# FFN up projection of an fp32 decoder trunk: 18 of 22 gate/linear tile pairs by seven block products in place of eight

## The reference

```
D_MODEL = 1024
SEQ = 512
DEPTH = 4
FFN_HIDDEN = -(-8 * D_MODEL // (3 * 256)) * 256
...
def swiglu(h, w_gate_up, w_down):
    g, u = jnp.split(h @ w_gate_up, 2, axis=-1)
    return (jax.nn.silu(g) * u) @ w_down
...
        x = x + swiglu(rmsnorm(x, ffn_norm[i]), ffn_w_gate_up[i], ffn_w_down[i])
```

## Time and profile before

| | |
|---|---|
| median of 3 runs | 2382.03 us (2381.8 to 2382.3) |
| profiled execution, span | 2380.3 us |
| TensorE busy | 2370.0 us, 100% of the span, 11768 matmuls |
| weight loads busy | 2002.1 us, 84% |
| VectorE busy | 1332.7 us, 56% |
| ScalarE busy | 899.4 us, 38% |
| GpSimd busy | 310.5 us, 13% |
| memory read | 208.68 MB, 89 GB/s over the span |

### The profile page before, as it was taken

The page is one execution under the profiler, slowest core; times in us unless marked ns, Lnnn a source line. Parts: engine busy times, 40 slices in busy tenths (PEclk is TensorE's granted clock), DMA queues, the critical chain, the costliest instruction groups (busy, mean ns, idle before and its releaser), DMA issues.

```text
span 2380.3 us, 33586 instructions
## 1 busy us (share of the span) xinstructions
PE 2370.0 (100%) x11768; PEld 2002.1 (84%) x11768; DVE 1332.7 (56%) x2199; ACT 899.4 (38%) x1376; POOL 310.5 (13%) x305
## 2 busy tenths in 40 slices
PE   9999999999999999999999999999999999999998
PEld 7899988888888888888888888888889998888887
DVE  8667765344465764443586644446756676534444
ACT  6267833222233432222233322223426773322223
POOL 2211140000040120000033000003420114000003
PEclk9999999999999999999999999999999999999999
DMA  4710023232233232322233223233370002223232
GB/s 165 224 46 2 2 69 108 88 101 93 99 105 106 89 106 91 103 97 97 97 99 106 97 91 104 89 106 105 121 208 27 2 2 89 97 89 106 89 105 89
DMA packets 64616, 220.58 MB, mean 93 GB/s; under 512 B 7680, under 2 KB 7808, under 8 KB 64512
## 3 DMA queue, kind: packets, MB, share of 16 engines
q1 hardware_dynamic: 58320, 208.59, 26.3%
q0 software_dynamic: 5184, 8.40, 1.6%
q10 hardware_dynamic: 1008, 2.21, 0.3%
HBM read 208.68 MB, written 2.10 MB: 89 GB/s over the span
## 4 chain that ended last, share of the span: by engine, by line
PE 99%; DVE 0%; DMA 0%; ACT 0%; SPq 0%; issue 0%; DVEq 0%
PE bank L1516 95%; PE bank L1796 3%; DMA x<-x_in 0%; PE bank L1826 0%; DVE branch L1281 0%; DVE big L1509 0%; SPq L434 0%; DVE rden L1276 0%; ACT L588 0%; DVE w_lo L939 0%; DVE rden L1278 0%; ACT w_hi L572 0%; PE bank L1700 0%; ACT xs_hi L581 0%; ACT xg L907 0%
## 5 line engine op out<-in xcount | busy, mean ns | idle before, releaser
L1516 PE MATMUL bank<-xs_hi,w_hi 128*128 128x512 f32 (+1 forms) x1808 | 708.9, 392 | 1.1 <-DVE xs_lo L947 0.5
L1516 PE MATMUL bank<-xs_lo,w_hi 128*128 128x512 f32 (+1 forms) x1808 | 703.3, 389 | 0.0
L1516 PE MATMUL bank<-xs_hi,w_lo 128*128 128x512 f32 x1792 | 697.3, 389 | 0.0
L939 DVE TENSOR_TENSOR w_lo<-raw,w_hi 128x1024 fp32r<-128x1024 f32 x369 | 469.7, 1276 | 230.7 <-ACT w_hi L572 226.3
L572 ACT ACTIVATE w_hi<-raw 128x1024 fp32r<-128x1024 f32 x372 | 390.8, 1051 | 432.6 <-PE bank L1516 231.7
L1516 PEld LDWEIGHTS bank<-xs_hi,w_hi 128*128 128x128 f32 (+1 forms) x1808 | 339.0, 188 | 74.4 <-DVE xs_lo L947 1.5
L1516 PEld LDWEIGHTS bank<-xs_lo,w_hi 128*128 128x128 f32 (+1 forms) x1808 | 338.4, 187 | 71.0 <-issue 1.0
L1516 PEld LDWEIGHTS bank<-xs_hi,w_lo 128*128 128x128 f32 x1792 | 336.4, 188 | 70.0
L1516 PE MATMUL bank<-hid_hi,w_hi 128*128 128x512 f32 x720 | 280.5, 390 | 0.0
L1516 PE MATMUL bank<-hid_lo,w_hi 128*128 128x512 f32 x720 | 280.1, 389 | 0.0
L1516 PE MATMUL bank<-hid_hi,w_lo 128*128 128x512 f32 x720 | 280.1, 389 | 0.0
(11 more groups left out here) (212 smaller groups left out, 2719.8 us busy)
## 6 DMA issues: line engine op xcount, KB each, us to landing
raw<-stream SPq DMA_DIRECT2D x371, 512.0 KB, 3.2
w_f<-stream SPq DMA_DIRECT2D x18, 512.0 KB, 3.5
hid_hi<-mix_hi POOLq DMA_DIRECT2D x32, 128.0 KB, 3.7
hid_lo<-mix_hi POOLq DMA_DIRECT2D x32, 128.0 KB, 3.1
out<-big SPq DMA_DIRECT2D x8, 256.0 KB, 2.9
x<-x_in ACTq DMA_DIRECT2D x4, 256.0 KB, 6.8
x<-x_in SPq DMA_DIRECT2D x4, 256.0 KB, 7.5
big<-consts SPq DMA_DIRECT2D x1, 664.0 KB, 11.0
```

Of the source, the lines that this page charges most:

```text
L939: nc.vector.tensor_tensor(w_lo[:, slot, :], raw[:, k, :], f32(w_hi[:, slot, :]), ALU.subtract).then_inc(w_lo_ready, counted(b))
L1516: return nc.tensor.matmul(out_, w, v, start=start, stop=stop)
```

## The change

The eight tokens-by-weights block products of a hidden tile (weights cut in two by input feature and in two as gate and linear; tokens cut in two by input feature and in two halves of 256 tokens) become the seven of Strassen's scheme in Winograd's form. The first four tiles of a layer stay as they were; the other 18 (`PAIRS` of 4, 7 and 7, in parts of 8, 7 and 7 tiles) go the new way. In four layers that is 72 tiles.

- Tokens: VectorE scales them by gain and `rrow` into `b32` (`scaled`), GpSimd makes four sums of 128x1024 (`token_sums`), and ScalarE and VectorE split sums and plain quarters into high and low parts. All this happens once a layer, among the four plain tiles.
- Weights: a pair's load is 128 x 2048 into `raw_a` or `raw_b`. VectorE makes four sums in three instructions (`pair_sums`), and both engines split seven blocks in four chunks (`pair_high`, `pair_low`), three of 1024 columns and one of 512.
- TensorE (`pair`): seven products of 12 matmuls of 256 columns. Some add onto a bank that holds an earlier product, of which ScalarE has copied the partial sum before (`snap`, into `part_sums`).
- VectorE and ScalarE: sums of the partial results into the four quarters (`lin`), Silu in two halves, product (`joined`), split of the hidden tile (`high`, `low`).
- The loops of the FFN are written out, and `first_tiles` orders the start of a layer by hand.

```diff
-PARTS = (8, 8, 6)
+PARTS = (8, 7, 7)
+FIRST_TILES = 4
+PAIRS = (4, 7, 7)
+H = 256
...
+PRODUCTS = ("s1", "s2", "a11", "s4", "s3", "a12", "a22")
...
+            def load_pair(l, p, j):
+                q = pair_at(l, p, j)
+                if j % 2 and j == 1:
+                    sp.wait_ge(w_lo_ready, plain_before(l, p))
+                elif j > 1:
+                    sp.wait_ge(sw_lo_ready, 4 * (q - 1))
...
+            def token_sums(l):
...
+                gp.wait_ge(scaled_ready, MT * l + 4)
+                nc.gpsimd.tensor_tensor(t1, b12, b11, ALU.subtract).then_inc(t_ready, 1)
+                gp.wait_ge(scaled_ready, MT * (l + 1))
+                gp.wait_ge(t_ready, 4 * l + 1)
+                nc.gpsimd.tensor_tensor(t2, b22, t1, ALU.add).then_inc(t_ready, 1)
+                nc.gpsimd.tensor_tensor(t3, b22, b12, ALU.add).then_inc(t_ready, 1)
+                gp.wait_ge(t_ready, 4 * l + 2)
+                nc.gpsimd.tensor_tensor(t4, b21, t2, ALU.subtract).then_inc(t_ready, 1)
...
+                    for j in range(count):
+                        q = pair_at(l, p, j)
+                        ahead = j + 1 < count
+                        if ahead:
+                            pair_high(l, p, j + 1, 0)
+                        else:
+                            down_high(l, p, 0)
+                        if j:
+                            high(j - 1)
+                        else:
+                            act.wait_ge(hid_lo_ready, t0)
+                        snap(q, 2, S1_DONE, sums_ready)
+                        if ahead:
+                            pair_high(l, p, j + 1, 1)
+                            pair_high(l, p, j + 1, 2)
...
+                        snap(q, 1, S2_DONE)
...
+                        snap(q, 0, A11_DONE, c21_ready)
+                        snap(q, 3, S3_DONE, c22_ready)
...
+            def pair_sums(l, p, j):
...
+                dve.wait_ge(pair_full[j % 2], 32 * (loads_before(q) + 1))
+                both = raw_q[:, :].rearrange("p (i c) -> p i c", i=4)
+                nc.vector.tensor_tensor(s32[:, 0:BW].rearrange("p (i c) -> p i c", i=2),
+                                        both[:, 3:4, :].broadcast_to([P, 2, S]), both[:, 0:3:2, :], ALU.subtract
+                                        ).then_inc(s_ready, 1)
+                dve.wait_ge(s_ready, 3 * q + 1)
+                nc.vector.tensor_tensor(s2, a11, s1, ALU.subtract).then_inc(s_ready, 1)
+                dve.wait_ge(s_ready, 3 * q + 2)
+                nc.vector.tensor_tensor(s4, a12, s2, ALU.subtract).then_inc(s_ready, 1)
...
+                        if not final:
+                            if k == 4:
+                                pair_sums(l, p + 1, 0)
...
+                            if k == 7:
+                                pair_sums(l, p + 1, 1)
...
+                    elif name == "s4":
+                        pe.wait_ge(snapped, 4 * q + 1)
...
+                    elif name == "s3":
+                        pe.wait_ge(snapped, 4 * q + 2)
...
+                    elif name == "a12":
+                        pe.wait_ge(snapped, 4 * q + 3)
...
+                    hi, lo = chunk(l, p, j, c)
+                    opens = name in ("s1", "s2", "a11")
+                    for k in range(4):
+                        w = hi[:, at + k * P:at + (k + 1) * P], lo[:, at + k * P:at + (k + 1) * P]
+                        end = mm3(dst[name][:, 0:H], w, token_part(name, k), opens and k == 0, k == 3, not opens)
+                    end.then_inc(product_done, 1)
```

More of the change, by code:

```diff
@@ L40 @@
 HIDDEN_TILES = 22
-PARTS = (8, 8, 6)
+PARTS = (8, 7, 7)
+TILES_AT = (0, 8, 15)
+FIRST_TILES = 4
+PAIRS = (4, 7, 7)
+PAIRS_AT = (0, 4, 11)
+LAYER_PAIRS = sum(PAIRS)
+H = 256
 BW = 1024
@@ L455, in loads @@
                         load(b, (b - plan.skipped(b)) % RAW)
-            at = RAW
-            for a, b0 in enumerate(plan.nsa_at):
-                end = plan.nsa_at[a + 1] if a + 1 < len(plan.nsa_at) else plan.blocks
-                loads(at, b0 + STATIC)
-                at = b0 + STATIC
-                pairs = (end - at) // RAW
-                with sp.Fori(0, pairs) as i:
-                    for k in range(RAW):
-                        load(i * RAW + (at + k), (at + k - plan.skipped(at)) % RAW)
-                at += pairs * RAW
-            loads(at, plan.blocks)
+            def load_pair(l, p, j):
[5 more added lines that the diff above has]
+                else:
+                    sp.wait_ge(sw_lo_ready, 4 * q)
+                for half in range(2):
+                    sp.dma_start(pair_raw(j)[:, bass.ts(half, BW)], pairs[q, :, bass.ts(half, BW)]
+                                 ).then_inc(pair_full[j % 2], 16)
+            at = RAW
+            for l in range(len(mixers)):
+                up = plan.ffn[l]
+                loads(at, up + 4)
+                load_pair(l, 0, 0)
+                loads(up + 4, up + 2 * FIRST_TILES)
+                for p, n in enumerate(PAIRS):
+                    for j in range(1, n):
+                        load_pair(l, p, j)
+                    down = plan.down_block(l, p)
+                    sp.wait_ge(sw_lo_ready, 4 * (pair_at(l, p, n - 1 - n % 2) + 1))
+                    loads(down, down + RAW)
+                    if p < len(PARTS) - 1:
+                        load_pair(l, p + 1, 0)
+                    loads(down + RAW, down + MT)
+                at = down + MT
             for k, (h, t) in enumerate(turned):
@@ L1020, in out_projection @@
                             split_after(b, slot, l)
+            def pair_sums(l, p, j):
+                q, raw_q = pair_at(l, p, j), pair_raw(j)
+                a11, a12 = raw_q[:, 0:S], raw_q[:, S:BW]
+                s3, s1, s2, s4 = (s32[:, bass.ts(i, S)] for i in range(4))
+                dve.wait_ge(pair_full[j % 2], 32 * (loads_before(q) + 1))
[7 more added lines that the diff above has]
+                nc.vector.tensor_tensor(s4, a12, s2, ALU.subtract).then_inc(s_ready, 1)
@@ new lines, in ffn, with amid @@
+            def ffn(l):
+                n, up = norm_of_ffn(l), plan.ffn[l]
+                def amid(k):
+                    if k == 2:
+                        norm(n)
+                project(up, up % RING, MT, xs, (xs_lo_ready, MT * n))
+                for b in range(up + 1, up + 2 * FIRST_TILES):
+                    project(b, b % RING, MT, xs, before=amid if b == up + 1 else None)
+                for p, (tiles, count) in enumerate(zip(PARTS, PAIRS)):
+                    for j in range(count):
+                        pair(l, p, j)
+                    down, t0 = plan.down_block(l, p), HIDDEN_TILES * l + TILES_AT[p]
+                    for k in range(MT):
+                        b = down + k
+                        project(b, b % RING, tiles, hid, (hid_lo_ready, t0) if k == 0 else None)
```

499 lines of the change are left out of this document (363 added, 136 removed).

## The result

The changed kernel takes **2435.8 us** (median of 4 runs, 2434.3 to 2439.1) against 2381.9 us for the kernel before on the same chip: a ratio of 1.0229, 95% interval 1.0214 to 1.0243. The forecast was 2406 with a range of 2362 to 2434. The sign was right and the size wrong: the loss is 54 us where 24 were forecast, 1.8 us beyond the range. Another case than the likeliest came true in part (the clock), and something that no case held (the ends of the parts).

What follows compares the result with a forecast made beforehand. The prediction took TensorE, busy 100%, to bound the kernel. Span 2380.3, less 57.6 for seven products, plus 12 for the steady loop and 70 for layer starts, gave 2404.7; with 1.7 from span to median, 2406 us, range 2362 to 2434.

Steps and rivals of the forecast that it cites:

- the likeliest: Forecast case: the first pair of each layer loses 14 to 23 us, giving 2392 to 2428 us; chance 0.55.
- the clock: Rival: TensorE idles before s4 of each first pair and the granted clock falls, giving 2422 us; chance 0.2.
- What bounds the kernel: Whole kernel before the change: TensorE, busy 100%, hardly waits; time taken off it shortens the end, new waits lengthen it.
- Term 1: Seven products on TensorE: 84 matmuls of 256 columns 0.12 us apart, 10.08 us a tile, 57.6 us gained.
- The rival of exposed loads: In the seven products, weight loads of 0.19 us are exposed or set the pace: 2750 us; 0.05 with the unforeseen.
- Term 2: Steady pairs: the loop through VectorE and ScalarE takes 10.3 us against TensorE's 10.08; 12 us lost, ends 0 and 35.
- Term 3: Start of each layer's FFN: VectorE's preparation delays s4 of pair 0; 17.5 us a layer, 70 lost, ends 28 and 91.
- Costed at nothing: Weight transfers, down blocks, the last tile's readiness at a part's end and ScalarE's work in a pair: no cost.
- (a): Rival at the layer start: GpSimd and ScalarE fill gaps, first pair costs 7.0 us a layer; 2352 us, chance 0.2.
- (b): Rival at s4 of each first pair: TensorE idles, the clock falls to 1.2 GHz; 16 us more, 2422, chance 0.2.
- (c): Rival in the seven products: weight loads are exposed or bound the pace; 2750 us, chance 0.05 with the unforeseen.
- (d): Rival: the change doesn't do what it says; excluded beforehand by the order rows' 6048 matmuls of 256 columns.

Runs made afterwards that it cites:

- e1_part_end: The change, with a11's and s3's snaps ahead of the third down block's high part in each part's last pair, its low part after the last sum; 2407.3 us.
- e7_more_vector: e1_part_end with VectorE's low part of the hidden tile written twice in every pair, one more instruction of 512 columns; 2416.6 us.
- e2_snaps_first: The change, with all four snaps of each layer's first pair ahead of the second pair's four chunks on ScalarE; 2445.8 us.
- e10_six_snaps: e1_part_end with six plain tiles a layer, VectorE's and ScalarE's layer-start work reordered, and pair 0's snaps of s1, s2, a11 ahead of pair 1's chunks; 2349.4 us.

## Why the prediction was right or wrong

**What bounds the kernel**: right. TensorE's waits, slow matmuls and small delays, 110 us more than before, less the 57.6 saved, are the 52 us between the spans.

**Term 1, seven products, -57.6**: right. In the steady pairs the matmuls start 0.12 us apart over hundreds in a row (a part of seven pairs is 588, 70.87 us in e1_part_end against 70.56), with their own weight loads all hidden. The rival of exposed loads fell: a run of 588 behaves as the four of the earlier trace rows. With it fell the rule of the Trainium skill that was set beside it (TensorE: Matmul & The Clock Gate, "The mechanism"), that a load overlaps a matmul only where the row groups differ: here the measurement decides. The same section of the Trainium skill also names a second way, a load into a background weight buffer. Which way these loads took, no run here shows.

**Term 2, steady loop, +12**: wrong in size, about +2.5, and that at the first pair of a part. The step that failed is "that makes the loop 10.3 us". The loop goes round in 9.93 us, of which 0.18 is a wait for ScalarE (forecast 0.3) and 9.75 is VectorE's own work (forecast 10.0): on the other side of TensorE's 10.08. The loop came out under the lower end of 10.0, whose loss had been put at 0, so the loss itself lay within the term's ends (0 and 35). e7_more_vector shows that the mechanism was right and the margin 0.15 us; VectorE is busy 87% in these parts (63.4 of 72.8), not the over 95% forecast.

**Term 3, layer start, +70**: +79. The walk found the right instruction, the right chain behind it and the right time within 1.3 us. That is partly luck, since two errors inside it nearly cancelled: GpSimd's sums last 2.4 us alone where the slope from 256 and 512 columns gave 1.66, and less of them counts. What it left out is the slow clock inside the first part: pair 0 ended at 423.2, not 421.1, and 1.9 us of that are slow matmuls behind s4.

**"Costed at nothing"**: this is the step that put the time outside the range. It had the ends of the parts at no cost, and they cost 28 us: with them mended the kernel takes 2407.3 us. It priced the tiles' readiness at a part's end, and loads by their landing times; it did not walk ScalarE's queue there, where a wait for a transfer stands ahead of two snaps. The same reading that found the chunk ahead of the snap in pair 0 would have found it. The missing question was which of ScalarE's instructions waits for something that is issued late.

**The rivals.** (a) fell: the first pair loses 19.7 us a layer, not under 10. (b) came true as a mechanism: the granted clock falls in each layer, though not at the wait before s4 alone. Priced at 16 us, it stands in the trace with 21 us of slow matmuls; how much of that would go with the clock alone is not shown (2.8 us in the one place that was tested alone, not clear of the noise; some of the rest is in the 28.5 of the part ends). (c) and (d) fell. 2406, less 9.5 for the loop, plus 9 for the layer start and 28 for the part ends, makes 2434, and the profiled execution took 2434.3. That the loop's error and the layer start's cancel is luck.

The sign hung on one thing, as the sum had it: what is saved by multiplying less (57.6) against the work that must be done before the first such multiplication. With more time for that work, the right queue order and the part ends mended, the seven products, now in 16 of 22 tiles, give 1.4%.

## What to carry to other kernels

Where an engine runs strictly in program order, walk its queue at every seam (first unit, last unit) and ask of each entry what it waits for and who stands behind it; a split that waits for a late transfer ahead of a cheap copy cost as much here as GpSimd's sums. A trick that trades TensorE's time for preparation on other engines must be sized at its start, by the time those engines have there, and not by their mean busy share. Mending one engine's order while another engine is late moves the wait (3 us gained at most); mended together with the other's, it gained 15 us, though a wait of 2.25 us came up behind it. And a wait can cost more than its length: where the clock falls with it, count the matmuls behind it at half speed.

## What the runs showed of the hardware that I had not expected

- Near waits of TensorE of 2 to 5 us there were, in most places, 10 to 20 matmuls at half the clock: 0.21 us apart for 256 columns in place of 0.12. Not in all: in the change, behind the waits of 3.8 us that ended at 380.3 and of 2.7 that ended at 404.5, the spacing stayed at the higher clock's. The fall needn't belong to the wait just ahead: in the change the clock was down from 406.1, and the 5 us wait before s4 began at 410.5. In the kernel before, without waits, the clock was up until the last 5 us.
- Two kernels whose waits sum to the same 86 us differed by 13.8 us in the one profiled execution of each, and 13.7 us of that are matmuls at half the clock (e2_snaps_first against the change; the medians are 10 us apart).
- A float32 multiply of 128 columns stands in the trace as two, 0.11 us apart at the higher clock and 0.21 at the lower; 14 of them last 4.0 us, 40 last 9.85.
- GpSimd's addition of two float32 tiles of 1024 columns takes 2.4 us where nothing holds it, and a VectorE instruction of two tiles that meets it takes 2.3 to 3.5 us in place of 1.22.
- Durations of VectorE's neighbouring instructions overlap by 0.08 us; only start distances add up to a loop.

What stays open: how much of the slow clock's time in the first two bursts of a layer is on the path (only the burst behind s4 was taken away alone, and in three layers of four), and whether five plain tiles would do better than six. Neither was tried, nor the two changes of e10_six_snaps one at a time.
